# Attention values with a base per half of the key rows and 256-column corners, in a two-layer float32 decoder on one core

## The reference, cut to what matters

```python
prev = jnp.concatenate([jnp.zeros_like(tb[:, :1]), tb[:, :-1]], axis=1)
...
diff = WINDOW + qi - s                       # s runs over 2 * WINDOW keys
valid = (diff >= 0) & (diff < WINDOW)
...
probs = jax.nn.softmax(jnp.concatenate([logits, sink], axis=-1), axis=-1)[..., :-1]
o = jnp.einsum("bnqkgd,...->...", probs, v_band)   # cut: probs (q, s) times values (s, d)
return (o * jax.nn.silu(z)) @ w_out
```

## Time and profile before

| | before |
|---|---|
| median of three runs | 2229.74 us |
| span of the profiled execution (the page gives no other time of it) | 2230.9 us |
| TensorE busy | 2163.5 us, 97% |
| VectorE busy | 1436.8 us, 64% |
| ScalarE busy | 1032.7 us, 46% |
| GpSimd busy | 1037.3 us, 46% |
| mean granted TensorE clock | 0.996 |

### The profile page before, as it was taken

How to read it: one execution, slowest core, us unless ns; L and a number is a source line. 1 busy time by engine, 2 the same in 40 slices (tenths; PEclk the granted TensorE clock), 3 DMA queues, 4 the chain that set the end, 5 groups by cost and what they waited for, 6 DMA issues and landing times.

```text
span 2230.9 us, 28791 instructions
## 1 busy us (share of the span) xinstructions
PE 2163.5 (97%) x10410; PEld 1808.6 (81%) x10410; DVE 1436.8 (64%) x1815; ACT 1032.7 (46%) x1898; POOL 1037.3 (46%) x636
## 2 busy tenths in 40 slices
PE   5999999999999999999999999999999999999998
PEld 4887778788888878888787888887888888888887
DVE  6966548757476864554974653867676657657764
ACT  4334445634545644445644445434444434434442
POOL 2556775845553865544684555440222232232222
PEclk9999999999999999999999999999999999999999
DMA  9888899785559795557876565989677797787554
GB/s 344 307 300 309 310 319 343 236 309 174 201 189 334 277 322 173 197 192 279 312 277 247 179 211 206 353 341 361 226 282 243 260 342 251 268 313 274 196 203 170
DMA packets 244782, 592.86 MB, mean 266 GB/s; under 512 B 20928, under 2 KB 96800, under 8 KB 244256
## 3 DMA queue, kind: packets, MB, share of 16 engines
q1 hardware_dynamic: 241680, 585.71, 72.8%
q10 hardware_dynamic: 2960, 5.30, 0.7%
HBM read 461.96 MB, written 119.54 MB: 261 GB/s over the span
## 4 chain that ended last, share of the span: by engine, by line
PE 74%; DMA 7%; POOL 6%; DVE 5%; ACT 3%; DVEq 2%; POOLq 1%; issue 1%; SPq 1%; ACTq 0%
PE ps L2272 22%; PE ps L2274 22%; PE ps L2273 22%; POOL w_lo L1110 3%; DMA w_raw<-in_a_w_in 2%; PE ps L2477 2%; POOL cbl L1129 1%; PE ps L2527 1%; PE ps L2526 1%; PE ps L2552 1%; DMA zo<-tt 1%; DVE yb L2018 1%; DMA w_raw<-a_weights_combined 1%; DMA r<-b_input 1%; ACT w_hi L1304 1%
## 5 line engine op out<-in xcount | busy, mean ns | idle before, releaser
L1110 POOL TENSOR_TENSOR w_lo<-w_raw,w_hi 128x1024 fp32r<-128x1024 f32 x244 | 650.4, 2684 | 568.8 <-ACT w_hi L1304 568.8
L1304 ACT ACTIVATE w_hi<-w_raw 128x1024 fp32r<-128x1024 f32 x260 | 271.7, 1057 | 413.8 <-DMA w_raw<-in_a_w_in 370.2
L2272 PE MATMUL ps<-h,w_hi 128*128 128x512 f32 x1024 | 403.2, 394 | 10.2 <-POOL w_lo L1110 9.4
L2274 PE MATMUL ps<-h,w_lo 128*128 128x512 f32 x1024 | 398.9, 390 | 0.0
L2273 PE MATMUL ps<-h,w_hi 128*128 128x512 f32 x1024 | 398.7, 389 | 0.0
L1249 POOL TENSOR_SCALAR_AFFINE_SELECT pt<-pt 128x512 fp32r<-128x512 f32 x128 | 82.2, 642 | 395.4 <-ACT pt L1666 338.9
L2272 PEld LDWEIGHTS ps<-h,w_hi 128*128 128x128 f32 x1024 | 192.2, 188 | 55.5 <-POOL w_lo L1110 14.7
L2274 PEld LDWEIGHTS ps<-h,w_lo 128*128 128x128 f32 x1024 | 192.2, 188 | 40.6
L2273 PEld LDWEIGHTS ps<-h,w_hi 128*128 128x128 f32 x1024 | 192.4, 188 | 38.9 <-issue 0.2
L2272 PE MATMUL ps<-r,w_hi 128*128 128x512 f32 x480 | 191.7, 399 | 3.8 <-ACT kvf L1608 2.3
L2274 PE MATMUL ps<-r,w_lo 128*128 128x512 f32 x480 | 187.7, 391 | 0.0
(11 more groups left out here) (268 smaller groups left out, 4636.8 us busy)
## 6 DMA issues: line engine op xcount, KB each, us to landing
w_raw<-in_a_w_in SPq DMA_DIRECT2D x256, 256.0 KB, 3.6
w_hi<-b_weights_split SPq DMA_DIRECT2D x104, 512.0 KB, 4.4
w_lo<-b_weights_split SPq DMA_DIRECT2D x104, 512.0 KB, 5.8
w_raw<-in_a_w_in SPq DMA_DIRECT2D x52, 512.0 KB, 4.9
w_raw<-in_a_w_out SPq DMA_DIRECT2D x48, 512.0 KB, 5.7
w_hi<-v_weights_combined SPq DMA_DIRECT2D x48, 512.0 KB, 4.0
w_lo<-v_weights_combined SPq DMA_DIRECT2D x48, 512.0 KB, 5.1
w_hi<-a_weights_combined SPq DMA_DIRECT2D x32, 512.0 KB, 6.3
```

Source lines behind the costliest of these rows:

```text
L1110: g.tensor_tensor(wlo[p][:, rows_], raw[p][:, rows_], whi[p][:, rows_].bitcast(F32), ALU.subtract).then_inc(w_lo, 1)
L1304: s_.activation(whi[p][:, rows_], raw[p][:, rows_], ACT.Copy).then_inc(w_hi, 1)
L2272: t_.matmul(dst_, stat[0], mov[0], start=start, stop=False)
L2274: return t_.matmul(dst_, stat[1], mov[0], start=False, stop=stop)
```

## The change

- **Values.** The base `vst` becomes one tile per block whose rows 0 to 63 are this block's values and whose rows 64 to 127 are the previous block's. That is wrong only in two corners: key rows 0 to 63 with queries 0 to 63 where s > q, and key rows 64 to 127 with queries 64 to 127 where s <= q. They are corrected by two matmuls of 256 columns (4 heads by 64 queries) on a tile `pe_`. High part and rest of a probability are stacked on the two halves of the 128 rows of `pe_`, and the differences are doubled over the halves in `edge_low` and `edge_up`.
- **Per step.** VectorE's rest (L2234) now signals `pt_all`; ScalarE, behind its four exponentials, waits for `pt_all` and copies the two corners of the rest across the partition halves (two copies of 64 rows by 256 columns, signal `pt_lo`). GpSimd drains, makes four selects of 64 rows by 256 columns in place of two of 128 by 512, and waits for its own `pt_masked`. TensorE waits for `pt_hi`, `pt_all` and `pt_masked` between the matmuls of `values` in place of `pt_masked` ahead of them.
- **Per group and kv head.** `kv_round` has 7 ScalarE operations in place of 3; `kv_rest` 7 VectorE operations in place of 3; `df` is 2 in place of 1; the copy of `vst` in `kv_shift` goes.
- **Waits and places.** ScalarE's wait on `xk_out[1]` and `hb_out[1]` moves from the write of `pt` to the exponentials of step 0, since `pp` now lies where `hbs` 1 is. `pt` shrinks to two tiles; `ot`, `obt`, the third `wh` and `keep` (gone) change places; a memset of `vst` goes.

```diff
-                for m, ready in ((0, pt_hi), (1, pt_lo)):
-                    pool.wait_ge(ready, a + 1)
-                    last = g.affine_select(out=pt[:, 2 + m].rearrange("p (h q) -> p h q", h=4),
...
+                high = pt[:, 0].rearrange("p (h q) -> p h q", h=4)
+                pool.drain()
+                pool.wait_ge(pt_hi, a + 1)
+                kept(pe_[64:P, 1], high[64:P, :, HEAD:P], True)
+                kept(pe_[0:64, 0], high[0:64, :, 0:HEAD], False)
+                pool.wait_ge(pt_lo, a + 1)
+                kept(pe_[0:64, 1], pe_[0:64, 1].rearrange("p (h q) -> p h q", h=4), True)
+                kept(pe_[64:P, 0], pe_[64:P, 0].rearrange("p (h q) -> p h q", h=4), False).then_inc(pt_masked, 1)
+                pool.wait_ge(pt_masked, a + 1)
...
-                s_.activation(vst[:, 1:5, kh, 0:HEAD], kvf[:, 1:5, cols_], ACT.Copy)
-                s_.activation(dst[:, :, kh, 0:HEAD], df[:], ACT.Copy).then_inc(kv_hi_done, 1)
+                s_.activation(vst[0:64, :, kh, 0:HEAD], kvf[0:64, 1:5, cols_], ACT.Copy)
+                s_.activation(vst[64:P, :, kh, 0:HEAD], kvf[64:P, 0:4, cols_], ACT.Copy)
+                for there in (slice(0, 64), slice(64, P)):
+                    s_.activation(edge_low[there, :, kh, 0:HEAD], df[0:64], ACT.Copy)
+                    last = s_.activation(edge_up[there, :, kh, 0:HEAD], df[64:P], ACT.Copy)
+                last.then_inc(kv_hi_done, 1)
...
-                    else:
-                        act.wait_ge(xk_out[1], 16 * 2)
-                        act.wait_ge(hb_out[1], 16 * 2)
                     s_.activation(pt[:, 0, :], bank(6), ACT.Copy).then_inc(pt_hi, 1)
                 if 0 <= a < ATT:
                     act.wait_ge(m_ready, a + 1)
                     if a >= 2:
                         act.wait_ge(pt_full, a - 1)
+                    elif a == 0:
+                        act.wait_ge(xk_out[1], 16 * 2)
+                        act.wait_ge(hb_out[1], 16 * 2)
...
+                if 0 <= a - 1 < ATT:
+                    act.wait_ge(pt_all, a)
+                    low = pt[:, 1, :].rearrange("p (h q) -> p h q", h=4).bitcast(F32)
+                    s_.activation(pe_[64:P, 0].rearrange("p (h q) -> p h q", h=4), low[0:64, :, 0:HEAD], ACT.Copy)
+                    s_.activation(pe_[0:64, 1].rearrange("p (h q) -> p h q", h=4), low[64:P, :, HEAD:P], ACT.Copy) \
+                        .then_inc(pt_lo, 1)
...
-                v.tensor_tensor(dst[:, :, kh, HEAD:P], df[:], dst[:, :, kh, 0:HEAD].bitcast(F32), ALU.subtract) \
-                    .then_inc(kv_lo_done, 1)
+                v.tensor_tensor(vst[64:P, :, kh, HEAD:P], kvf[64:P, 0:4, cols_], vst[64:P, :, kh, 0:HEAD].bitcast(F32),
+                                ALU.subtract)
+                for there in (slice(0, 64), slice(64, P)):
+                    v.tensor_tensor(edge_low[there, :, kh, HEAD:P], df[0:64], edge_low[0:64, :, kh, 0:HEAD].bitcast(F32),
+                                    ALU.subtract)
+                    last = v.tensor_tensor(edge_up[there, :, kh, HEAD:P], df[64:P],
+                                           edge_up[64:P, :, kh, 0:HEAD].bitcast(F32), ALU.subtract)
+                last.then_inc(kv_lo_done, 1)
...
-                pe.wait_ge(pt_masked, a + 1)
                 if a >= 1:
                     pe.wait_ge(o_done, a)
+                pe.wait_ge(pt_hi, a + 1)
                 t_.matmul(bank(7), vst[:, blk, kh, :], pt[:, 0, :], start=True, stop=False)
+                pe.wait_ge(pt_all, a + 1)
                 t_.matmul(bank(7), vst[:, blk, kh, :], pt[:, 1, :], start=False, stop=False)
-                t_.matmul(bank(7), dst[:, blk, kh, :], pt[:, 2, :], start=False, stop=False)
-                t_.matmul(bank(7), dst[:, blk, kh, :], pt[:, 3, :], start=False, stop=True).then_inc(pv_full, 1)
+                pe.wait_ge(pt_masked, a + 1)
+                by_query = bank(7).rearrange("p (h q) -> p h q", h=4)
+                t_.matmul(by_query[:, :, 0:HEAD], edge_low[:, blk, kh, :], pe_[:, 0, :], start=False, stop=False)
+                t_.matmul(by_query[:, :, HEAD:P], edge_up[:, blk, kh, :], pe_[:, 1, :], start=False, stop=True) \
+                    .then_inc(pv_full, 1)
```

More of the change, by code:

```diff
@@ L442, in yoco_kernel @@
         zg = place("zg", v_at, [KT, T], F32)
-        pt = place("pt", v_at + 16 * K, [4, 512], F32R)
-        pp = place("pp", v_at + 24 * K, [2, 4, P + 1], F32)
+        pt = place("pt", v_at + 16 * K, [2, 512], F32R)
+        pp = place("pp", v_at + 20 * K, [2, 4, P + 1], F32)
+        edge_low = place("edge_low", v_at + 24 * K + 64, [NC, KVH, P], F32R)
+        pe_ = place("p_edge", v_at + 28 * K + 64, [2, 4 * HEAD], F32R)
+        obt = place("obt", v_at + 30 * K + 64, [2, P], F32)
         xs = place("xs", x_at, [NC, D], F32)
@@ L460, in yoco_kernel @@
         ks = place("ks", gt, [KVH, 2, 5 * P], F32R)
-        vst = place("vst", gt + 10 * K, [5, KVH, P], F32R)
-        ot = place("ot", gt + 15 * K, [2, P], F32)
+        vst = place("vst", gt + 10 * K, [NC, KVH, P], F32R)
         wst = place("wst", sp_at, [GROUPS, P], F32)
@@ L468, in yoco_kernel @@
         bsh = place("bsh", sp_at + 8 * K, [GROUPS * P], F32)
-        dst = place("dst", sp_at, [NC, KVH, P], F32R)
+        edge_up = place("edge_up", sp_at, [NC, KVH, P], F32R)
         kw = place("kw", sp_at + 4 * K, [T], F32)
@@ L477, in yoco_kernel @@
         gate_b = place("gate_b", gb_at, [D], F32)
-        wh = [place(f"wh{n}", w_at, [T], F32) for n, w_at in enumerate((wh_at, wh_at + 2 * K, v_at + 29 * K + 512))]
+        wh = [place(f"wh{n}", w_at, [T], F32) for n, w_at in enumerate((wh_at, wh_at + 2 * K, gt + 14 * K))]
         tt = [place(f"tt{n}", ga_at + 2 * K * n, [T], F32) for n in range(2)]
@@ L513, in yoco_kernel @@
         ident = place("ident", region(512), [P], F32)
-        ones = place("ones", region(512), [P], F32)
-        keep = place("keep", region(512), [P], F32)
+        ones_at = region(1024)
+        ones = place("ones", ones_at, [P], F32)
+        ot = place("ot", ones_at, [2, P], F32)
         prev = place("prev", region(512), [P], F32)
@@ L1076, in _ @@
             g.memset(ones[:], 1.0).then_inc(pool_pro, 1)
-            g.memset(keep[:], 1.0)
             g.memset(prev[:], 1.0)
@@ L1245, in mask, with kept @@
             def mask(a):
[L1247 to L1253 removed]
+                def kept(there, in_, low):
+                    heads = there.rearrange("p (h q) -> p h q", h=4)
+                    if low:
+                        return g.affine_select(out=heads, in_=in_, compare_op=ALU.is_ge, fill=0.0, base=0,
+                                               pattern=[[0, 4], [1, HEAD]], channel_multiplier=-1)
+                    return g.affine_select(out=heads, in_=in_, compare_op=ALU.is_gt, fill=0.0, base=0,
+                                           pattern=[[0, 4], [-1, HEAD]], channel_multiplier=1)
+                high = pt[:, 0].rearrange("p (h q) -> p h q", h=4)
[7 more added lines that the diff above has]
+                pool.wait_ge(pt_masked, a + 1)
             def normalise(a):
@@ L2125, in kv_shift @@
                     v.tensor_copy(ks[:, kh, :, 0:P], ks[:, kh, :, 4 * P:5 * P].bitcast(F32))
-                    v.tensor_copy(vst[:, 0, kh, :], vst[:, 4, kh, :].bitcast(F32))
                 dve.wait_ge(kv_copied, at("kv_copied", g, 4))
-                v.tensor_tensor(df[:], kvf[:, 1:5, cols_], kvf[:, 0:4, cols_], ALU.subtract).then_inc(d_f, 1)
+                v.tensor_tensor(df[0:64], kvf[0:64, 0:4, cols_], kvf[0:64, 1:5, cols_], ALU.subtract)
+                v.tensor_tensor(df[64:P], kvf[64:P, 1:5, cols_], kvf[64:P, 0:4, cols_], ALU.subtract).then_inc(d_f, 1)
             def kv_rest(g, kh):
```

15 lines of the change are left out of this document (6 added, 9 removed).

## The result

| | before | after |
|---|---|---|
| median of the runs, us | 2231.89 (4 runs) | 2261.43 (4 runs, 2257.68 to 2265.06) |
| ratio | | 1.0134, 95% interval 1.0119 to 1.0149 |
| span of the profiled execution, us | 2230.9 | 2259.4 |
| mean granted TensorE clock | 0.996 | 0.992 |

The runs of the kernel before are the three named above and a fourth of 2234.69 us. The change costs 29.5 us (1.3%); the forecast was 12, with 2256 as the upper end of the range. The sign was right and the size was not. The span has grown by 28.5 us.

A forecast was written before the change was run, and what follows sets the result against it. TensorE, busy 97% of the span, was taken as the bound. Terms -14 (shorter matmuls) + 10 + 9 + 3 + 2 + 2 = +12 us gave a median of 2242 us, range 2221 to 2256.

The forecast's parts named there:

- kh = 1: Longer `kv_round` and `kv_rest` in the slots of steps 3, 19, 35, 51 make TensorE wait: 10 us in sum.
- the moved wait: Wait for the `hbs` 1 store, moved to step 0's exponentials, delays the attention's start: 3 us, bounds 0 and 8.
- kh = 0: `kv_rest` longer by 1.7 us delays the next logits and values in steps 11, 28, 29, 46: 9 us in sum.
- `kvf` with the gate: Two `kvf` waits and the gate wait directly behind the exponentials each grow by 0.78: 2.3 us.
- the clock: Rival: TensorE's clock falls behind waits of 2 to 3 us, 1.7 each at five places, 2251 us; chance 0.10.
- step 11: Values wait 2.7 us: 0.46 plus 0.44 available, 1.65 needed, and the exponentials' end moves by 1.7 + 0.2.
- steps 3, 19 and 51: Preparation for kh = 1 exceeds the 1.2 us to spare; TensorE waits 2.5, 1.6 and 1.6 us.
- the 2 us of other steps: Steps about a microsecond late for ropes and queries waiting for ScalarE: 2 us together, bounds 0 and 4.
- Steps 28 and 29: `kv_round` ahead of L1666 costs 1.7 us in step 28, the longer `kv_rest` 2.2 in step 29.
- All hidden: Rival: all new work is hidden except 1 to 3 us, gain comes through, 2216 to 2222 us; chance 0.16.
- VectorE and ScalarE catch up: Rival: catching up and TensorE's own waits halve the 26 us of loss, 2229 us, no change; chance 0.21.
- Corner matmuls as long as before: Rival: output cut into runs makes the corner matmuls take as long as before, 2256 us; chance 0.03.

The follow-up runs named there:

- kernel 3: Changed kernel without ScalarE's two copies, GpSimd's selects moving the rests across the partition halves themselves: median 2240.25 us, ratio 1.0046 to the kernel before.
- kernel 2: Kernel before with `kv_round` and `kv_rest` lengthened to seven operations each, two of each writing a spare tile, `df` in two: 2247.08 us, ratio 1.0077.
- kernel 4: Changed kernel with GpSimd's selects moving the rests and ScalarE's two copies still made, into a tile nobody reads: 2250.91 us, ratio 1.0099 to the kernel before.
- the second profile: Profile of the changed kernel run once more, nothing altered: median 2260.88 us, ratio 1.0134 to the kernel before.
- kernels 1: Changed kernel with three operations for seven in `kv_round` and `kv_rest`, both corner matmuls reading `edge_low` (value sums not right): 2235.56 us, ratio 1.0022 to before.
- kernel 5: Changed kernel with the preparation's corner operations moved to later slots, two at a time, nothing left out: 2237.81 us, ratio 1.0034 to the kernel before.
- experiment 8: Changed kernel again (2260.88 us); with GpSimd moving the rests and corner operations in later slots (2224.30 us); that with the wait put back as well (2222.60 us).
- kernel 6: Kernel before with only its two `dst` matmuls cut to 256 columns, half their terms left out: 2222.39 us, ratio 0.9959.

## Why the prediction was right and wrong

**Right.** The corner matmuls (0.12, forecast 0.11), the selects (0.42, forecast 0.41), the copies (0.42), `kv_rest` for kh = 1 (3.3, forecast 3.2), the moved wait (3.6 alone, 3.9 in the trace, forecast 3), the steps in which TensorE would stall and that quiet steps hide the chain. An operation on half the rows costs as much as one on all rows: in `kv_rest` for kh = 1 each of the seven starts only when the one ahead is over, 0.70 behind the first and 0.43 behind the others. For kh = 0 the first two both start at row 0, and there the second starts 0.60 us behind a first of 0.67 (1518.11 and 1518.71). The Trainium skill (VectorE: DVE Perf Modes, "Two Vector instructions with no wait between them") has an instruction held until all earlier ones are done when a start quadrant changes; both cases agree with it.

**Wrong: how late a late step makes TensorE.** Three terms of the sum were too small, kh = 1 (10, measured 17.8), kh = 0 (9, measured 11.6) and `kvf` with the gate (2.3, measured 8.0), and the clock, which is contained in these measured figures, was not in the sum at all. Four steps of the working failed.

1. *How late the exponentials are.* For step 11 I had "the end moves by 1.7 + 0.2". Before, the last exponential ended 5.74 us behind the transposes that open the slot, and it ends 8.47 behind them now: 2.7 later, not 1.9. That is not ScalarE's copies: without them it is 8.44 (kernel 3), and with the longer preparation in the kernel before 8.25 (kernel 2). `kv_rest` for this step takes 4.2 us against 2.2 before, 2.1 more in place of 1.7, since in both kernels one or more of its operations are drawn out; the rest of the difference stays open. In steps 3, 19 and 51 the copies do count: the end lies 7.33, 6.64 and 7.33 us behind the transposes in the changed kernel and 6.45, 5.67 and 5.97 in kernel 3. By kernel 4 ScalarE's time comes to 12 us over all steps; I had it at 2.3, the 2 us of other steps and a part of the 10. Steps 28 and 29 were put too high: 3.9, measured 1.6 and, in the second profile, 2.8.
2. *The corner chain and the time to spare.* In steps 3, 11, 19, 28, 29, 35 and 51 the third value matmul starts 1.86 us behind the end of the exponentials (2.37 in step 46), where I had 1.65; so a quiet step has 1.0 us to spare, not 1.2. Step 11, forecast at 2.7:

```profile
1675.18 0.47 PE L2584 MATMUL ps<-pt,vst 128*128 128x512 f32 x1 [2.81 <-issue]
1675.48 0.40 PE L2586 MATMUL ps<-pt,vst 128*128 128x512 f32 x1
1676.62 0.45 PE L2589 MATMUL ps<-p_edge,edge_low 128*128 128x256 f32 x1 [0.74 <-POOL p_edge L1249]
...
1677.09 0.63 PE L2295 MATMUL ps<-r,w_hi 128*128 128x512 f32 x1
1677.52 0.63 PE L2296 MATMUL ps<-r,w_hi 128*128 128x512 f32 x1
```

   The first matmul waits 2.97 us for `o_done` and the third 0.91 more for the corners, then come some 1.5 us of slow matmuls. The two waits are one hold of 3.9 us, and the corners, which come last, set its end. `o_done` comes 0.3 us behind the exponentials in the kernel before too, and there it already held step 11 by 0.29 us; I read it in the earlier trace rows as the largest wait and counted the 0.46 us up to that held matmul as time to spare. So 0.8 us of lateness, 0.2 of chain and 0.3 of spare time that was not there make the 3.9 out of the 2.7. In steps 3, 19 and 51 the hold is 2.7, 2.1 and 2.8 us (forecast 2.5, 1.6 and 1.6), in kernel 3 it is 0.9, 0.5 and 0.5, in kernels 1 and 5 nothing. That is what lateness and chain do when they share one spare time: 5.6 us in these three steps go with either cause, most of the 8 us of experiment 8.
3. *The clock was a rival at 0.10 and belonged in the sum.* It and the forecast were not two cases: where the forecast's waits of 2 to 4 us come true, the clock falls behind most of them in this kernel. The price was right (1.7 each; seven of the stretches measured 1.2 to 1.7), the number of places was eight, not five: 10 us over the kernel before. Forecast plus this rival would have been 2251. The Trainium skill (TensorE: Matmul & The Clock Gate, Part 1) calls the throttled clock the default, which activity releases. The eight stretches fit that as far as each stands behind a wait and ends while TensorE works; why the same wait of 3.55 us has one behind it in one execution and none in the other, no run here shows.
4. *`kvf`, 0.78 each forecast, 3.3 and 3.2 measured.* 0.86 is ScalarE's copies directly ahead of it. The rest is a chain I did not walk: GpSimd's selects of step 25, behind those copies, meet VectorE's scaling of 1024 columns and take 0.84 and 1.30 us in place of 0.41; `r2u`, the next scaling and the exponentials follow 0.7 us later; and behind the wait of 2.88 us the clock falls, 1.5 us (in the second profile it does not, and the place costs 1.8 us in all).

```profile
1816.70 0.84 POOL L1247 TENSOR_SCALAR_AFFINE_SELECT p_edge<-p_edge 64x256 fp32r<-64x256 f32 x1 [2.27 <-ACT p_edge L1692]
1817.59 1.30 POOL L1249 TENSOR_SCALAR_AFFINE_SELECT p_edge<-p_edge 64x256 fp32r<-64x256 f32 x1
1818.97 1.04 POOL L1265 TENSOR_TENSOR pp<-pp,rden 128x512 f32<-128x512 f32 x1
1820.27 0.26 POOL L1280 TENSOR_SCALAR r2u<-ssq,r2t 128x1 f32<-128x1 f32 x1 [0.25 <-issue]
```
```profile
1829.47 0.47 PE L2295 MATMUL ps<-r,w_hi 128*128 128x512 f32 x1 [2.88 <-ACT kvf L1615]
```

   Without the copies (kernel 3) the two waits are 2.7 us together, against 2.3 before. That the contention alone makes the 0.7 was not tried.

**The other rivals.** *All hidden* is refuted as to this kernel; but the mechanism I gave it, the spare time of ordinary steps, is what kernel 5 uses: the forecast did not ask whether the operations could stand elsewhere. *VectorE and ScalarE catch up* is refuted: behind a late step TensorE is late for good, and only 2.7 us come back, from waits for transfers. *Corner matmuls as long as before* is refuted by their rows. The gain itself had a rival that I did not name: transfers that are just in time, which keep back some 4 of 13 us in kernel 6 (by its interval 0.3 to 7).

## What to carry to other kernels

Where an engine's queue is the bound only now and then, the question about an added operation is not what it costs but in which slot it stands: the same eight corner operations (four on ScalarE, four on VectorE, per token group and kv head) cost 22 us ahead of a deadline and, as far as can be told, some 3 us a few slots later. For each late step, take the one thing that comes last (here the corners, 1.86 us behind the exponentials), add up its lateness and its chain and take off the spare time once; check that the spare time of the kernel before is not itself the end of a wait. Two changes that draw on the same spare time are dearer together than apart. Where the forecast itself makes TensorE wait as long as in these rows, put the price of the clock into the range: in the changed kernel it came behind most such waits, and not always the same ones, in kernel 3 only at the start. And charge an operation that goes into every slot to every chain that runs through that queue. A copy that only moves data between partition halves is best given to an operation that must touch the data anyway, where that costs as little as GpSimd's selects here.

## What was not expected of the hardware

- GpSimd's select reads one half of the partitions and writes the other at the same 0.42 us as within a half (kernel 3).
- ScalarE's copies of 64x256 do not overlap: each starts 0.01 us behind the end of the one ahead. Those from tiles take 0.42 us, whether they change the partition half (`p_edge`, 0.43 apart) or keep it (`vst`, 0.40 to 0.42); those from `ps` take 0.38 and lie 0.39 apart. So the length goes with what they read and not with the move.
- The table load of the exponentials was at 1531.02 before, ahead of its data. With the moved wait it starts only when that wait ends, so that 1.28 us more lie on the path. Changed kernel, start of the attention: issue of the store, ScalarE, and TensorE's logits of step 1 (before: the earlier trace rows):

```profile
1533.40 0.49 SPq L931 DMA_DIRECT2D b_input<-hbs  x1
```
```profile
1542.72 1.28 ACT L1683 ACT_TABLE_LOAD   x1 [11.18 <-DMA b_input<-hbs]
1544.02 0.37 ACT L1683 ACTIVATE pp<-ps,negm 128x129 f32<-128x129 f32 x1
```
```profile
1545.62 0.55 PE L2549 MATMUL ps<-ks,qs 128*128 128x256 f32 x1 [4.49 <-issue]
```
